# A hybrid mLSTM and attention layer in split fp32: x turned by plain transposes for six of its eight token tiles, high parts written ahead of copies, and the second weight pair's P1 ahead of the first pair's P7

## The reference

```python
def hybrid_layer(x, pre_w, w_in, ...):
    h = rmsnorm(x, pre_w)
    proj = h @ w_in                       # 1024 x 13320 columns
    q_m, k_m, v_m, o_m, z_m, if_pre, q_a, k_a, v_a, z_a, g_m, g_a = split(proj)
    q_m, k_m = split(silu(causal_depthwise_conv(concat(q_m, k_m), conv_w, conv_b)))
    hm = mlstm_chunkwise(q_m, k_m / 16, v_m, i_pre, log_f)      # 4 heads of 256, chunks of 128
    hm = rmsnorm(hm * sigmoid(o_m)) * m_norm_w * silu(z_m)
    for (window, dilation) in ((128, 1), (512, 4), (2048, 16)): # 4 heads of 128 per group
        outs, maxes, dens = dilated_window_attention(rope(q_a), rope(k_a), v_a, ...)
    att = combine(outs, maxes, dens) * silu(z_a)
    merged = sigmoid(g_m) * (hm @ w_pm) + sigmoid(g_a) * (att @ w_pa)
    return x + rmsnorm(merged @ w_out, post_w)
```

## Time and profile before

| | |
|---|---|
| time, median of 3 runs | 1398.48 us (1397.7 to 1400.67) |
| time of the profiled execution | 1400.15 us |
| its span in the profile | 1398.4 us |
| busy: PE, PEld, DVE, ACT, POOL | 1364.3, 1135.0, 784.8, 642.7, 570.3 us |
| share of PE in the chain that ended last | 85% |
| granted TensorE clock, mean | 0.993 of full speed |

### The profile page before, as it was taken

The page is one execution under the profiler, slowest core; times in us unless marked ns, Lnnn a source line. Parts: engine busy times, 40 slices in busy tenths (PEclk is TensorE's granted clock), DMA queues, the critical chain, the costliest instruction groups (busy, mean ns, idle before and its releaser), DMA issues.

```text
span 1398.4 us, 18850 instructions
## 1 busy us (share of the span) xinstructions
PE 1364.3 (98%) x6500; PEld 1135.0 (81%) x6500; DVE 784.8 (56%) x1253; ACT 642.7 (46%) x1321; POOL 570.3 (41%) x408
## 2 busy tenths in 40 slices
PE   8899999999999999989999998999999999989998
PEld 6688888888888888878878887887888888878786
DVE  4865338236543734967666664764544442977632
ACT  7544543543444455345545445444544553533421
POOL 5453436344443534654335344343333544444000
PEclk9999999999999999999999999999999999999999
DMA  6113242324233323464443534335253354965521
GB/s 189 50 46 93 55 84 88 94 48 128 68 84 70 105 56 68 137 186 127 110 141 83 166 108 110 117 120 154 67 169 108 90 182 166 333 207 162 199 91 60
DMA packets 211358, 165.02 MB, mean 118 GB/s; under 512 B 33296, under 2 KB 187440, under 8 KB 211264
## 3 DMA queue, kind: packets, MB, share of 16 engines
q1 hardware_dynamic: 211264, 163.81, 39.7%
HBM read 117.41 MB, written 40.08 MB: 113 GB/s over the span
## 4 chain that ended last, share of the span: by engine, by line
PE 85%; DVE 6%; DMA 4%; issue 2%; SPq 1%; ACT 1%; DVEq 0%; POOLq 0%; POOL 0%; ACTq 0%
PE proj L1224 63%; PE proj L1169 5%; PE proj L1152 3%; PE keep L1269 2%; PE bank L1248 2%; PE bank L1334 2%; DMA neg_g<-g_spill 2%; PE keep L1325 2%; PE bank L1297 1%; PE bank L1257 1%; PE bank L1330 1%; DVE tmp L1958 1%; DVE share L1907 1%; PE bank L1280 1%; DMA x_sb<-x_in 1%
## 5 line engine op out<-in xcount | busy, mean ns | idle before, releaser
L1066 POOL TENSOR_TENSOR w_lo<-raw,w_hi 128x512 fp32r<-128x512 f32 x164 | 236.1, 1441 | 439.4 <-ACT w_hi L1428 439.4
L1224 PE MATMUL proj<-hi_T,w_hi 128*128 128x512 f32 x832 | 337.9, 406 | 6.1 <-DVE lo_T L2034 4.4
L1224 PE MATMUL proj<-hi_T,w_lo 128*128 128x512 f32 x832 | 325.1, 391 | 0.0
L1224 PE MATMUL proj<-lo_T,w_hi 128*128 128x512 f32 x832 | 324.1, 390 | 0.0
L1224 PE MATMUL proj<-hi_B,w_hi 128*128 128x512 f32 x624 | 256.7, 411 | 7.2 <-issue 3.7
L1224 PE MATMUL proj<-hi_B,w_lo 128*128 128x512 f32 x624 | 245.7, 394 | 0.0
L1224 PE MATMUL proj<-lo_B,w_hi 128*128 128x512 f32 x624 | 245.3, 393 | 0.0
L1066 POOL TENSOR_TENSOR w_lo<-s_sb,w_hi 128x512 fp32r<-128x512 f32 x104 | 153.3, 1476 | 183.7 <-ACT w_hi L1428 183.2
L1224 PEld LDWEIGHTS proj<-hi_T,w_hi 128*128 128x128 f32 x832 | 156.4, 188 | 41.1 <-issue 7.9
L1224 PEld LDWEIGHTS proj<-hi_T,w_lo 128*128 128x128 f32 x832 | 156.1, 188 | 34.1
L1224 PEld LDWEIGHTS proj<-lo_T,w_hi 128*128 128x128 f32 x832 | 156.6, 188 | 30.3
(11 more groups left out here) (239 smaller groups left out, 2021.3 us busy)
## 6 DMA issues: line engine op xcount, KB each, us to landing
raw<-w_in SPq DMA_DIRECT2D x95, 512.0 KB, 6.0
m_spill<-stage SPq DMA_DIRECT2D x16, 1024.0 KB, 4.0
chunk<-m_spill SPq DMA_DIRECT2D x32, 512.0 KB, 4.2
gate_spill<-stage SPq DMA_DIRECT2D x8, 1024.0 KB, 4.0
gst<-gate_spill SPq DMA_DIRECT2D x32, 256.0 KB, 3.1
share<-share_spill SPq DMA_DIRECT2D x12, 512.0 KB, 5.2
x_sb<-x_in SPq DMA_DIRECT2D x8, 512.0 KB, 6.7
hm_spill<-stage SPq DMA_DIRECT2D x4, 1024.0 KB, 9.2
```

Source lines behind the costliest of these rows:

```text
L1066: TT(w_lo_ring[k % RING][:], src, w_hi_ring[k % RING][:].bitcast(F32), ALU.subtract).then_inc(lo_pool, 1)
L1224: mm = pe.matmul(acc(p, which), w[:, kt, :], m[:, kt, :], start=(first and kt == 0 and w is wh and m is h_hi[b]), stop=(kt == 3 and w is w ...
```

## The change

It has six parts.

1. x tiles 0 to 5 are multiplied in place by the power (tiles 0 to 3 on DVE, 4 and 5 on POOL) and turned with `pe.transpose` against the identity. Tiles 6 and 7 keep `diag`. The gate columns of w_in come from an array that the host has laid out tile by tile (`w_if`), and ACT writes their high part from it directly. Squares of tile 5 move from ACT to DVE.
2. ACT writes the high part of a bank first, DVE the low part, and the copy `b_sb` is taken last. All of `second_half` stands behind P2.
3. P1 of the second pair stands ahead of P7 of the first. Its low weights come from POOL and those of P7 from DVE.
4. Head 0's chunks start at steps 177, 180, 183 ... instead of 175, 178, 182 .... The first `chunk_in` of heads 1 to 3 stands one step earlier, and so do the second convolution of a q or k pair from pair 24 on and its spill.
5. The seven PSUM tensors become two, and the products by w_pa use four pairs of banks in place of two; the pairs of w_pm wait for earlier ones of them.
6. The output tiles take four pairs of banks in turn.

```diff
     seq = [(first, "P1")]
     for p in range(first, first + count):
-        seq += [(p, n) for n in ("P2", "P6", "P5", "P7")]
+        seq += [(p, n) for n in ("P2", "P6", "P5")]
+        follow = [(p, "P7")]
         if p + 1 < first + count:
-            seq.append((p + 1, "P1"))
+            follow.insert(0 if p == 0 else 1, (p + 1, "P1"))
+        seq += follow
         seq += [(p, "P4"), (p, "P3")]
...
-    for h, (first, gap) in enumerate(((175, 3.5), (203, 4.375), (238, 4.375), (273, 3.5))):
+    for h, (first, gap) in enumerate(((177, 3.25), (203, 4.375), (238, 4.375), (273, 3.5))):
...
-        ready = 7 * pair_of["mo", h] + 11
+        ready = 7 * pair_of["mo", h] + (10 if h else 11)
...
-            for j, a in ((1, 7), (0, 12)):
+
+            late = at + 12 < SECOND_TMP
+            for j, a in ((1, 7), (0, 12 if late else 11)):
...
-            sp_late[at + 17].append(("spill", p))
+            sp_late[at + (17 if late else 16)].append(("spill", p))
...
+        def pa_slot(t):
+
+            return (side, side, proj, proj, proj, proj, side, side)[t][:, t % 2, :]
+
         def y_slot(t):
-            return proj[:, t % 2, :]
+            return (side, proj)[t // 2 % 2][:, t % 2, :]
...
-                    sp.dma_start(ifw[:], w_in[:, C_IF:C_IF + 2 * MH].rearrange("(k p) c -> p k c", p=P)
-                                 ).then_inc(start_in, 16)
-                if t == 5:
+                    sp.dma_start(ifw[:], w_if).then_inc(start_in, 16)
+                if t == 6:
...
+            def scale(t):
+                reciprocal_root(t)
+                g.wait_ge(x_rs, t + 1)
+                nc.gpsimd.tensor_scalar(x_sb[:, t, :], x_sb[:, t, :], ssq[:, NT + t:NT + t + 1], None, ALU.mult
+                                        ).then_inc(x_norm, 1)
...
             g.wait_ge(g_ready, 2)
+            for t in range(4):
+                reciprocal_root(t)
+            scale(4)
+            low(0)
+            scale(5)
+            low(1)
             g.wait_ge(start_in, 16 * NSTART)
-            for t in range(6):
-                reciprocal_root(t)
-            low(0)
             for t in range(6, NT):
-                reciprocal_root(t)
-            low(1)
+                diagonal(t)
...
                 if p == NP and name in ("P1", "P2"):
-                    pe.wait_ge(pa_done, KT - 1 if name == "P1" else KT)
+                    pe.wait_ge(pa_done, 5 if name == "P1" else 6)
...
-                pe.wait_ge(x_norm, t + 1)
+                pe.wait_ge(x_scaled, t + 1)
                 for kt in range(KT):
-                    mm = pe.matmul(ht1_bank[kt][:, t * P:(t + 1) * P], x_sb[:, t, kt * P:(kt + 1) * P], diag[:, t, :],
-                                   start=True, stop=True)
+                    mm = pe.transpose(ht1_bank[kt][:, t * P:(t + 1) * P], x_sb[:, t, kt * P:(kt + 1) * P], ident[:])
...
-                for kt in {0: (0, 4, 1, 5), 1: (2, 6, 3, 7)}.get(k, ()):
+                for kt in HT2_ORDER if k == 1 else ():
                     second_half(kt)
...
+            def scale(t):
+                dve.wait_ge(x_rs, t + 1)
+                TS(x_sb[:, t, :], x_sb[:, t, :], ssq[:, NT + t:NT + t + 1], None, ALU.mult).then_inc(x_scaled, 1)
+
             for t in range(4):
                 mean_square(t)
...
+                scale(t)
```

More of the change, by code:

```diff
@@ L139, in slot_tiles, with hybrid_kernel @@
     return g, out, place
-def hybrid_kernel(nc, x, w_in, w_pm, w_pa, w_out, b_gate, conv_wt, conv_bt, pre_wt, m_wt, post_w,
+def hybrid_kernel(nc, x, w_in, w_if, w_pm, w_pa, w_out, b_gate, conv_wt, conv_bt, pre_wt, m_wt, post_w,
                   c_ident, c_mask, c_tril, c_rope, out):
@@ L528, in hybrid_kernel @@
         pb = [proj[:, i // 2, i % 2 * 512:i % 2 * 512 + 512] for i in range(4)]
[L529 to L530 removed]
+        side = ctx.enter_context(nc.psum_tensor("side", [P, 2, 1024], F32))
+        bank = [side[:, i // 2, i % 2 * 512:i % 2 * 512 + 512] for i in range(BANKS)]
+        keep = side[:, 1, 512:1024]
         def acc(p, which):
             return pb[{"a": p % 2, "b": 2, "c": 3}[which]]
[L536 removed]
+        ht1_bank = [pb[0], pb[3], bank[0], pb[2], bank[1], bank[2], keep, pb[1]]
+        COPY_ORDER = (0, 1, 3, 4, 5, 6, 7, 2)
         HT2_ORDER = (0, 4, 1, 5, 2, 6, 3, 7)
[L538 removed]
+        ht2_bank = dict(zip(HT2_ORDER, [pb[2], bank[1], bank[2], keep, pb[1], pb[2], bank[1], bank[2]]))
         att_dram = nc.dram_tensor("att_spill", [AOUT, S], F32).ap()
@@ L1346, in _ @@
             pe.wait_ge(zero_done, 1)
-            for i in range(6):
+            for i in range(4):
                 pe.matmul(keep[:], snap[0][:, 0:P], snap[0][:], start=True, stop=True)
@@ L1365, in second_half @@
                 for t in range(4):
-                    pe.wait_ge(x_norm, 5 + t)
-                    mm = pe.matmul(b[:, t * P:(t + 1) * P], x_sb[:, 4 + t, kt * P:(kt + 1) * P], diag[:, 4 + t, :],
-                                   start=True, stop=True)
+                    pe.wait_ge(x_norm, t + 1)
+                    columns, turned = b[:, t * P:(t + 1) * P], x_sb[:, 4 + t, kt * P:(kt + 1) * P]
+                    if t < 2:
+                        mm = pe.transpose(columns, turned, ident[:])
+                    else:
+                        mm = pe.matmul(columns, turned, diag[:, 4 + t, :], start=True, stop=True)
                 mm.then_inc(pe_ht, 1)
@@ L1494, in h_high @@
                 A(h_hi[b][:, j, :], h_sum[b][:, j, :], ACT.Copy).then_inc(h_hi_done, 1)
-            for t in range(4):
-                square(t)
-            act.wait_ge(if_ready, 1)
-            A(iw[:], iw_raw[:], ACT.Copy).then_inc(iw_hi_done, 1)
-            act.wait_ge(start_in, 16 * NSTART)
-            for t in range(4, 6):
-                square(t)
+            square(0)
+            act.wait_ge(start_in, 16 * NSTART)
+            act.wait_ge(g_ready, 2)
+            for c in range(2):
+                ins = A(iw[:, :, c:P:32], ifw[:, :, c * MH:(c + 1) * MH], ACT.Copy)
+            ins.then_inc(iw_hi_done, 1)
+            for t in range(1, 5):
+                square(t)
+            first_high(0)
+            first_high(1)
             high(0)
-            for kt in range(4):
-                first_half(kt)
+            first_copy(0)
+            first_high(2)
+            first_high(3)
             high(1)
+            first_copy(1)
             for kt in range(4, KT):
-                first_half(kt)
+                first_high(kt)
+            for kt in COPY_ORDER[2:]:
+                first_copy(kt)
+            after(0)
             second_half(0)
             second_half(1)
+            high(2)
             h_high("T2", 0, 2)
-            after(0)
+            high(3)
+            h_high("T2", 1, 4)
             second_half(2)
-            h_high("T2", 1, 4)
-            high(2)
+            h_high("T2", 2, 6)
             second_half(3)
-            h_high("T2", 2, 6)
-            high(3)
             h_high("T2", 3, 8)
@@ L1522, in _ @@
             high(4)
+            high(5)
+            for j in range(4):
+                h_high("B22", j, 8)
             after(2)
@@ L1525, in _ @@
                 h_high("T3", j, 9 + j)
-            high(5)
             high(6)
-            after(4)
+            after(5)
             for j in range(4):
                 h_high("T4", j, 13 + j)
-            for j in range(4):
-                h_high("B22", j, 8)
-            ACT_EARLY, HIGH_EARLY = (2, 4), 6
+            ACT_EARLY, HIGH_EARLY = (2, 5), 6
             def piece(it):
@@ L2059, in _ @@
                 h_low("T1", j, 4 + j + 1, h_ready["T1"])
-            low(4)
+            low(5)
             after(1)
@@ L2178, in _ @@
                         piece(it)
-                if 4 < k + LEAD < NK and seq[k + LEAD][1] in LOW_DVE:
+                if 5 < k + LEAD < NK and seq[k + LEAD][1] in LOW_DVE:
                     low(k + LEAD)
```

89 lines of the change are left out of this document (48 added, 41 removed).

## The result

The changed kernel takes 1378.19 us (median of 4 runs, 1377.67 to 1379.48); before beside it took 1399.16 us. The ratio is 0.985 (95% interval 0.9834 to 0.9868): 1.5% faster, 21.0 us by the medians. The forecast was 1371.6 us, a gain of 26.9: the time lies in the stated range of 1368 to 1380 us, but 3.7 us above the forecast's own range of 1368.5 to 1374.5 us, which had the chance of 0.60. The profiled execution took 1377.68 us, its span is 1375.9 us (22.5 us less), and PE is busy for 1352.1 us of it.

What follows compares the result with a forecast made beforehand. PE, busy 1364.3 of 1398.4 us, was taken to bound the kernel. Head starts 18.3, banks 3.7 and opening 4.9 made 26.9 us off, forecast 1371.6 us (own range 1368.5 to 1374.5, chance 0.60; wide range 1368 to 1380).

Steps and rivals of the forecast that it cites:

- the opening rival: Opening: P1 starts and stays at the 1.2 GHz level through P2, so it gives next to nothing; 1375.9 us, chance 0.16.
- the signs: Expected in the trace: no `neg_g` wait over 1 us, clock 1.00 from some 30 us, first pair's P4 ending 5 us earlier.
- Head starts, 18.3 us: First chunks of the mLSTM heads: PE's `neg_g` waits go, 12.0 us, and the low clock behind them, 6.3 us.
- Banks at the end, 3.7 us: First two products by w_pm: PE's waits of 1.58 and 2.10 us for DVE's `gst`, through the banks, both go.
- It just fits, by 1.0 us: P7 by w_pm, fifth product, comes at 1234.5; DVE ends its low weights at 1233.5, so no wait.
- The rival of up to 1.6 us: Products by w_pm: P7 waits for DVE in place of P1 and P2; up to 1.6 us back, 1373.2, chance 0.05.
- Opening, 4.9 us: Parts 1 to 3, up to P4 of the first pair: four savings of 1.2, 1.9, 0.7 and 1.1 us; bounds 1.5 and 7.5.
- Its first step: First product, behind POOL's `w_lo`: tile 4 takes tile 5's place in the chain, start at 17.5, 1.2 us earlier.
- The second: PE in `second_half`: 16 of 32 fp32 matmuls become transposes, 1.9 us less work.
- The third: Inside P1: high and low parts ahead of copies remove PE's 0.68 us wait for `lo_B`, 0.7 us.
- The fourth: DVE's sum S3, 1.77 us beside POOL's T2 low parts where its like take 0.68: POOL is through earlier, 1.1 us.
- The best case, 1367.5 us: More gain than forecast, with DVE unhindered in the opening: 1367.5 us, chance 0.04.

Runs made afterwards that it cites:

- P7 first: The changed kernel with the first pair's P7 put ahead of the second pair's P1 again: 1378.59 us, ratio 0.9841 to before.
- DVE scales: The changed kernel with x tiles 4 to 7 scaled on DVE, all eight tiles turned by transposes, no scaling or diagonal on POOL: 1376.71 us, ratio 0.9834.
- PSUM alone: The kernel before the change with only the PSUM banks part (output product, w_pm and output tiles in turn): 1400.69 us, ratio 0.9990.
- both with the old opening: The kernel before the change with the head starts and the PSUM part, without the new opening: 1381.78 us, ratio 0.9859.
- w_lo first: The changed kernel with POOL's low parts of the first and second weights ahead of scaling x tiles 4 and 5: 1381.37 us, ratio 0.9857.
- sum late: The changed kernel with POOL's first weight sum of the second pair held until ACT's last T4 high part: 1379.75 us, ratio 0.9847.

## Why the prediction was right, and where it was wrong

The range held because it took in the opening rival, whose reason is only half right: that the time lies in it is in part luck. The forecast's own sum missed by 5.9 us in the gain, nearly all of it in two of its three terms. Two of the signs failed as well: the clock was not 1.00 from 30 us on (0.53 over 54.2 to 57.8), and P4 of the first pair ended 0.56 us earlier, not 5.

- **Head starts, 18.3 us: right.** 18.05 alone in the time, 19.0 in the trace. The chunk ahead of the weights and the whole 6.3 us of clock came as worked out.
- **Banks at the end, 3.7 us: the term was right, its cover was not.** "It just fits, by 1.0 us" is the step that failed (its 4 x 2.8 is 11.2, not 11.0, which would make it 1.2): it took DVE to end P7's low weights when it had, at its old durations. PE comes 3.7 us earlier, and with it POOL's low part and sum, which before came behind DVE's; so DVE's sum S4 and low weights take 1.77 and 1.75 us where they took 0.68 each. The rival of up to 1.6 us named the place; it cost 2.3 in each of the seven traces with the new banks and the old place of B22, and about 1.7 more in the four in which the clock fell. That both go when one line is moved is shown; that POOL is what slows DVE here is read from the rows, and tested only in the opening.
- **Opening, 4.9 us: mis-sized, it is 0.6 in the trace at the gates, and nothing that can be told from none in the time.** Its first step, 1.2 us from an earlier first product, took POOL's multiplication at 1.9 us; it is 2.85, and the power ahead of it 1.46 beside DVE's sum of squares, where others take 0.55. The first product came 0.5 us later. The second, 1.9 us of PE's work saved by transposes, is real, but PE only waits the longer. The third, 0.7 for the wait inside P1, went back in the 0.65 us ahead of P2. The fourth came true (S3 0.69 for 1.77 us), and was lost again in the T1 low parts (3.60 us for four, 2.48 before) beside POOL. The error under them is adding PE's and DVE's savings although the opening ends by one chain, DVE's T sums, whose start moved 1.9 us back when all of `second_half` went behind P2; that the chain still ended 1.67 us earlier is mostly due to the T2 and T4 low parts, which the sum does not have. Of these 1.67 us the clock behind PE's longer wait took 1.1, a term that the sum does not have either.
- **The opening rival had the right size, 1375.9 with the other terms whole, for a reason half right.** P1 did run at the 1.2 GHz level for some 4 us, and most of P4 too, behind its wait. Yet giving the clock back would not have freed P4 from DVE: with P1 started at 17.27 and a clock of 1.00 over 17.3 to 22.3 us, PE waited 3.10 us all the same. By the Trainium skill, TensorE: Matmul & The Clock Gate, Part 4, transposes do not count as work for the clock as matmuls do. In after the last matmul ahead of the transposes ends at 7.68 us, the clock stays at 1.00 over 8.5 to 16 us, with nothing but transposes up to 14.5, and it is 0.50 only in and behind the 4.75 us of idling that follow; so the trace does not bear that out.
- The best case, 1367.5 us, does not follow from the opening's own upper bound: 7.5 for 4.9 gives 1369.0.
- The sum of what was shown: 18.3 (19.0 in the trace), 1.8 at the end, 0.6 in the opening. That is 20.7 to 21.4 us against 26.9, with 21.0 measured. The trace has 1.1 us more between the gates and the last input pair than the kernel with the head starts alone; where it comes from is open.

## What to carry to other kernels

When a wait of PE goes, PE comes sooner to every later deadline of the same queue, and the other engines that follow PE move too, perhaps onto that queue's work: write down that queue up to the next deadline at its durations beside them, and put nothing ahead of it that is needed later. Savings on two engines do not add where one of them closes the stage; find the first instruction of the closing chain and ask whether the change starts it earlier or later. Price a wait of a few us together with the low clock that may follow it (1.6 to 3.0 us where it fell behind the head starts and P7), and as a chance, since the same wait does not always bring it.

## What the runs showed of the hardware

- The same wait of 2.30 us at P7 by w_pm left the clock at 1.00 in three traces (after, P7 first, DVE scales) and brought it to 0.77 to 0.79 over 7 to 8 us in four (PSUM alone, both with the old opening, w_lo first, sum late). Why is open. This, the `gst` wait and the arrival of x may make much of the spread of one kernel's runs, up to 7.7 us; with one trace of each kernel that is not shown.
- An fp32 multiplication of 128x1024 by a column takes 0.75 us on DVE and 2.85 on POOL in after (3.83 once, in w_lo first).
- POOL's power of one column takes 0.55 us alone and 1.46 beside DVE's sum of squares; a DVE sum of 128x512 takes 0.64 us alone (half of the pair's 1.28) and 1.74 beside POOL's (half of 3.47).
